# A one-core encoder layer: the value projection turned from token-major to feature-major, and the last two down steps of the last block taken token tile by token tile

## The reference

```python
h = rmsnorm(x, g_pre_mix)
q, k, v, u, g = split_projection(h, w_in)            # q 1024, k 128, v 128, u_a/u_b 1024 each, gates 2048
attn = sink_attention(q, band(k), band(v), rel_bias, valid, sink)   # window 128 + own chunk of 64, 2 kv heads
conv = silu(layernorm(depthwise_conv31(u) + b_dw)) @ w_conv_out
x = x + rmsnorm((g[0] * attn + g[1] * conv) @ w_out, g_post_mix)
h = rmsnorm(x, g_pre_ffn)
y = x + rmsnorm((silu(h @ w_ffn_gate) * (h @ w_ffn_up)) @ w_ffn_down, g_post_ffn)
```

## Time and profile before

| | |
|---|---|
| median of 3 runs | 3476.5 us (3476.41 to 3479.43) |
| the profiled execution | 3481.69 us |
| its span, first to last instruction | 3479.9 us |
| PE busy | 3326.8 us (96% of the span) |
| DVE, ACT, POOL busy | 46%, 29%, 10% |
| mean granted TensorE clock | 0.968 of full |

### The profile page before, as it was taken

The page is one execution under the profiler, slowest core; times in us unless marked ns, Lnnn a source line. Parts: engine busy times, 40 slices in busy tenths (PEclk is TensorE's granted clock), DMA queues, the critical chain, the costliest instruction groups (busy, mean ns, idle before and its releaser), DMA issues.

```text
span 3479.9 us, 42929 instructions
## 1 busy us (share of the span) xinstructions
PE 3326.8 (96%) x17118; PEld 2804.2 (81%) x17118; DVE 1597.9 (46%) x2873; ACT 993.2 (29%) x1830; POOL 358.2 (10%) x422
## 2 busy tenths in 40 slices
PE   7999889999999999999999999999999998899997
PEld 6777668878787878888787878888799987799985
DVE  5977645545785642003594552003397554300012
ACT  2536432224244421003144432002223532200021
POOL 0620000000161000000061000000044000100000
PEclk9999789999999999999999999999999997999998
DMA  7754257777653345555553344555554321355542
GB/s 235 297 221 175 86 194 293 285 277 288 218 182 133 109 157 175 189 199 200 206 194 133 117 148 161 192 193 201 193 178 160 110 86 61 138 182 170 179 147 104
DMA packets 177894, 623.29 MB, mean 179 GB/s; under 512 B 20592, under 2 KB 28080, under 8 KB 177184
## 3 DMA queue, kind: packets, MB, share of 16 engines
q1 hardware_dynamic: 176736, 620.15, 50.6%
q10 hardware_dynamic: 960, 0.40, 0.0%
HBM read 481.13 MB, written 139.44 MB: 178 GB/s over the span
## 4 chain that ended last, share of the span: by engine, by line
PE 71%; issue 6%; DVE 4%; POOL 2%; ACT 2%; DMA 2%; SPq 0%; DVEq 0%; POOLq 0%; ACTq 0%
PE PS L695 42%; PE PS L749 6%; PE PS L751 6%; PE PS L750 6%; PE PS L731 2%; PE PS L821 2%; POOL y L640 1%; DVE PS L1333 1%; PE PS L809 1%; DMA w_hi<-hi_dram 1%; PE PS L810 1%; PE PS L811 1%; PE PS L838 1%; PE PS L839 1%; PE PS L840 1%
## 5 line engine op out<-in xcount | busy, mean ns | idle before, releaser
L695 PE MATMUL PS<-h_hi,w_hi 128*128 128x512 f32 (+1 forms) x3288 | 1052.0, 353 | 18.2 <-DVE u L1542 10.8
L695 PE MATMUL PS<-h_hi,w_lo 128*128 128x512 f32 (+1 forms) x3288 | 1053.3, 353 | 0.0
L695 PE MATMUL PS<-h_lo,w_hi 128*128 128x512 f32 (+1 forms) x3288 | 1043.7, 350 | 0.0
L695 PEld LDWEIGHTS PS<-h_hi,w_hi 128*128 128x128 f32 x3288 | 579.1, 189 | 100.3 <-issue 15.7
L695 PEld LDWEIGHTS PS<-h_lo,w_hi 128*128 128x128 f32 x3288 | 579.1, 189 | 90.8 <-issue 2.2
L695 PEld LDWEIGHTS PS<-h_hi,w_lo 128*128 128x128 f32 x3288 | 579.1, 189 | 81.2
L1333 DVE SCALAR_TENSOR_TENSOR PS<-u,dw,PS 128x512 f32<-128x512 f32 (+1 forms) x696 | 485.8, 767 | 2.9
L1685 DVE TENSOR_TENSOR f<-PS,tmp 128x512 f32<-128x512 f32 (+1 forms) x88 | 61.6, 700 | 669.6 <-PE PS L695 650.7
L640 POOL TENSOR_TENSOR y<-y,prod 128x512 f32<-128x512 f32 (+1 forms) x240 | 289.8, 1239 | 405.9 <-ACT prod L1103 405.9
L749 PE MATMUL PS<-w_hi,f_hi 128*128 128x512 f32 x748 | 297.9, 398 | 5.8 <-DVE f L1685 5.4
L751 PE MATMUL PS<-w_hi,f_lo 128*128 128x512 f32 x748 | 295.8, 395 | 0.0
(11 more groups left out here) (185 smaller groups left out, 4096.8 us busy)
## 6 DMA issues: line engine op xcount, KB each, us to landing
w_lo<-lo_dram SPq DMA_DIRECT2D x372, 512.0 KB, 4.5
w_hi<-hi_dram SPq DMA_DIRECT2D x372, 512.0 KB, 3.6
w_raw<-in_w_stream SPq DMA_DIRECT2D x124, 512.0 KB, 3.9
hi_dram<-w_hi SPq DMA_DIRECT2D x124, 512.0 KB, 4.0
lo_dram<-w_lo SPq DMA_DIRECT2D x124, 512.0 KB, 4.0
x<-in_x_prompt SPq DMA_DIRECT2D x4, 2048.0 KB, 10.7
out_y_prompt<-x SPq DMA_DIRECT2D x4, 2048.0 KB, 7.1
xs<-in_x_prompt SPq DMA_DIRECT2D x12, 512.0 KB, 5.4
```

Source lines behind the costliest of these rows:

```text
L695: last = nc.tensor.matmul(PS[:, k0 + off, 0:n], w, x[:, k, c0:c0 + n], start=first and k == 0, stop=stop and k == KT - 1)
```

## The change

**Step 25** becomes a `feature_major` step like its neighbours. ACT copies its result (features on partitions) from PSUM to `tmp[:, 1]`; PE turns it with one transpose for each token tile (`turn_values`) into PSUM banks 6 and 7; ACT and DVE then take `v_hi` and `v_lo` from there. The turn stands behind the matmuls of step 26 in blocks 0 to 2. In the ext block banks 6 and 7 hold conv accumulators, so it stands behind step 29, after a wait for all taps. The sums of `kwin` move with it from iteration 26 to iteration 30 of DVE, and to another place in SBUF (that of `prod`, so they wait for POOL's last addition); their stores move from SP's iteration 28 to 31, and the wait for these goes from DVE (step 30) to ACT (second attention unit).

**Steps 122 and 123 of the ext block** are held back and run together in `down_tail`: for each token tile its 6 matmuls of step 122, then its 6 of step 123. `d_done` releases ACT's square of each tile when that tile is complete, and `store_y` issues one DMA for each tile.

```diff
-        kwin = at("kwin", R_sc, [P, 2, P])
-        kwin_s = at("kwin_s", R_sc + 2 * P * 4, [P, 2, P])
+        kwin = at("kwin", R_pt, [P, 2, P])
+        kwin_s = at("kwin_s", R_pt + 2 * P * 4, [P, 2, P])
...
+        def turn_step(b):
+            return S_A + 3 if ext(b) else S_A
...
             def store_y(b):
-                m = post_tile(b, tiles(b) - 1, 1)
-                sp.wait_ge(pn_ok, m + 1)
+                if ext(b):
+                    for tt in range(4):
+                        sp.wait_ge(pn_ok, post_tile(b, tt, 1) + 1)
+                        r0 = b * T + tt * P
+                        sp.dma_start(y_prompt[r0:r0 + P, :], x1[:, tt, :]).then_inc(y_out, 16)
+                    sp.wait_ge(pn_ok, post_tile(b, 4, 1) + 1)
+                    sp.dma_start(y_sample, x1[SR:P, 4, :]).then_inc(y_out, 16)
+                    return
...
-                    if ext(b) and s == S_A + 2:
+                    if ext(b) and s == turn_step(b) + 2:
                         sp.wait_ge(win_ok, 4)
...
-                result_out(pe, b, s - 2)
+                if s == S_A + 1:
+                    pe.wait_ge(v_sb_ok, b + 1)
+                else:
+                    result_out(pe, b, s - 2)
...
-            def values_of(b, s):
...
+            def down_tail(b):
+                for tt in range(tiles(b)):
+                    for s in (NS - 2, NS - 1):
+                        dd = s - S_D
+                        if tt == 0:
+                            weights(G(b, s))
+                            pe.wait_ge(flo_ok, b * FT + dd + 1)
+                        for kk in range(2):
+                            last = token_products(b, s, S_D, f_hi[:, dd % 2], f_lo[:, dd % 2], (0, 1), HALF_D,
+                                                  kk, tt)
+                        if tt == tiles(b) - 1:
+                            last.then_inc(w_used, 1)
+                    if tt < tiles(b) - 1:
+                        last.then_inc(d_done, 1)
+
+            def turn_values(b):
+                pe.wait_ge(v_sb_ok, b + 1)
+                for tt in range(tiles(b)):
+                    last = nc.tensor.transpose(PS[:, 6 + tt // 4, (tt % 4) * P:(tt % 4 + 1) * P],
+                                               tmp[:, 1, tok0(b, tt):tok0(b, tt) + P], ident_sb[:])
+                last.then_inc(vt_done, 1)
...
-                    if s < S_A - 1:
+                    if s < S_A:
                         if b or s >= 2:
                             feature_major(b, s, h_hi, h_lo, groups(b))
-                    elif s == S_A - 1:
-                        values_of(b, s)
                     elif s < first_unit(b):
                         feature_major(b, s, h_hi, h_lo, groups(b))
+                        if s == turn_step(b):
+                            if ext(b):
+                                pe.wait_ge(conv_step, (b + 1) * NTAP)
+                            turn_values(b)
...
                     if kind == "v":
-                        zv = PS[:, zbank(b, r), :].rearrange("p (t a d) -> p t a d", t=4, a=2)
+                        A(over(b, tmp[:, 1, 0:c]), z(b, r), ACT.Copy).then_inc(v_sb_ok, 1)
+                    if r == turn_step(b):
+                        act.wait_ge(vt_done, b + 1)
                         if ext(b):
-                            zw = PS[:, zbank(b, r) + 1, 0:P].rearrange("p (a d) -> p a d", a=2)
-                            A(v_hi[:, 5, 0:3:2, :], zw, ACT.Copy)
-                        A(v_hi[:, 1:5, 0:3:2, :], zv, ACT.Copy).then_inc(kv_hi_ok, 1)
+                            A(v_hi[:, 5, 0:3:2, :], PS[:, 7, 0:P].rearrange("p (a d) -> p a d", a=2), ACT.Copy)
+                        A(v_hi[:, 1:5, 0:3:2, :], PS[:, 6, :].rearrange("p (t a d) -> p t a d", t=4, a=2),
+                          ACT.Copy).then_inc(kv_hi_ok, 1)
...
+                            if n == 1 and ext(b):
+                                act.wait_ge(win_out, 16 * 6)
...
                 for tt in range(tiles(b)):
+                    if ext(b) and tt < tiles(b) - 1:
+                        act.wait_ge(d_done, tt + 1)
+                    else:
+                        act.wait_ge(w_used, G(b, NS - 1) + 1)
                     post_squares(b, tt, 1)
...
                         if ext(b):
-                            dve.wait_ge(z_dve, by_dve(b, r))
+                            dve.wait_ge(z_dve, by_dve(b, S_A - 1))
+                            dve.wait_ge(prod_used, NB * NPROD)
...
-                            dve.wait_ge(win_out, 16 * 6)
                         dve.wait_ge(mu_done, b + 1)
```

More of the change, by code:

```diff
@@ L197, in build @@
         o_done, w_gain_ok = sem("o_done"), sem("w_gain_ok")
+        d_done = sem("d_done")
         sq0_ok = sem("sq0_ok")
@@ L217, in build @@
         kv_hi_ok, hist_ok = sem("kv_hi_ok"), sem("hist_ok")
+        v_sb_ok, vt_done = sem("v_sb_ok"), sem("vt_done")
         dve_chain, pool_chain, act_chain = sem("dve_chain"), sem("pool_chain"), sem("act_chain")
@@ L518, in store_y @@
             def store_y(b):
-                m = post_tile(b, tiles(b) - 1, 1)
-                sp.wait_ge(pn_ok, m + 1)
+                if ext(b):
[6 more added lines that the diff above has]
+                    return
+                sp.wait_ge(pn_ok, post_tile(b, tiles(b) - 1, 1) + 1)
                 sp.dma_start(y_prompt[b * T:(b + 1) * T, :].rearrange("(t p) d -> p t d", p=P),
                              x1[:, 0:4, :]).then_inc(y_out, 16)
-                if ext(b):
-                    sp.dma_start(y_sample, x1[SR:P, 4, :]).then_inc(y_out, 16)
             def load_x0(tt):
@@ L582, in _ @@
             store_y(NB - 1)
-            sp.wait_ge(y_out, 16 * (NB + 1))
+            sp.wait_ge(y_out, 16 * (NB - 1 + 5))
             sp.wait_ge(win_out, 16 * 8)
@@ L776, in out_tail @@
                         last.then_inc(o_done, 1)
-            def values_of(b, s):
-                g, k0 = G(b, s), zbank(b, s)
-                weights(g)
-                result_out(pe, b, s - 2)
+            def down_tail(b):
                 for tt in range(tiles(b)):
[L784 to L791, removed]
+                    for s in (NS - 2, NS - 1):
[16 more added lines that the diff above has]
+                last.then_inc(vt_done, 1)
             def scores(b, n):
@@ L903, in _ @@
                         if ln == 3 and ext(b):
-                            pe.wait_ge(conv_step, (b + 1) * NTAP)
                             channel_means(b, ypieces, BY_TAPS + BY_POOL, True, True)
                         if ln == 4:
+                            result_out(pe, b, S_A - 1)
                             channel_squares(b, ypieces)
@@ L968, in _ @@
                             pe.wait_ge(hf_ok, first_norm(b + 1, tiles(b + 1) - 1) + 1)
+                        if ext(b) and s >= NS - 2:
+                            if s == NS - 1:
+                                down_tail(b)
+                            continue
                         pe.wait_ge(flo_ok, b * FT + dd + 1)
@@ L1523, in _ @@
                     kind = KINDS[r] if r >= 0 else None
-                    if kind in BY_DVE:
+                    if kind in BY_DVE and kind != "v":
                         dve.wait_ge(w_used, G(b, r) + 1)
@@ L1548, in _ @@
                            ALU.subtract).then_inc(z_dve, 1)
-                    if kind == "v":
+                    if r == turn_step(b):
                         dve.wait_ge(kv_hi_ok, 2 * b + 2)
                         if ext(b):
-                            zw = PS[:, zbank(b, r) + 1, 0:P].rearrange("p (a d) -> p a d", a=2)
+                            zw = PS[:, 7, 0:P].rearrange("p (a d) -> p a d", a=2)
                             TT(v_lo[:, 5, 0:3:2, :], zw, v_hi[:, 5, 0:3:2, :].bitcast(F32), ALU.subtract)
-                        zv = PS[:, zbank(b, r), :].rearrange("p (t a d) -> p t a d", t=4, a=2)
+                        zv = PS[:, 6, :].rearrange("p (t a d) -> p t a d", t=4, a=2)
                         TT(v_lo[:, 1:5, 0:3:2, :], zv, v_hi[:, 1:5, 0:3:2, :].bitcast(F32),
```

1 line of the change is left out of this document (removed).

## The result

The changed kernel takes 3432.9 us, median of 4 runs (3429.4 to 3437.6), against 3476.5 before: a ratio of 0.9876, 95% interval 0.9859 to 0.9893, or 43.6 us less. The forecast was 34.6 us less, 3441.9 us, with a range from 3438.

A forecast was written before the change was run, and what follows sets the result against it. PE, busy 96% of the span, was taken to bound the kernel. Values steps 14.1 + 6.8 = 20.9 us and tail 13.7 us sum to 34.6 us, from 3476.5 to 3441.9 us, range 3438 to 3448.

The forecast's parts named there:

- Sum: Whole kernel: values-step gain 20.9 plus tail gain 13.7 gives 34.6 us less, 3441.9 us from the median.
- Part A, blocks 0 to 2: Values step: 96 matmuls (10.66 us) become 24 (5.52 us) plus four transposes (0.43 us), gain 4.71 us a block.
- Ext block: Its values step: 13.34 us removed, 6.01 us and five transposes (0.53 us) added, gain 6.80 us.
- both covers: At the ext block's turn: taps finish 7.8 us before PE arrives; PE's means hide the window sums with 2 us to spare.
- Transposes: The 17 new ones in the values steps: 0.106 us each by starts in the trace, against the skill's some 275 ns.
- rival 3: New transposes don't overlap and run one behind the other: 4.1 us more, 3446.0 us; chance 0.05.
- Part B: Tail: last two down steps by token tile with five stores, 13.7 us less at the end of the span.
- the last store: Tail: the final 128 KB store, with nearly empty queues, was taken at 2.3 us, where it had landed in 6.5.
- the 0.4 us in that sum: Tail: added because POOL makes the last tile's factors beside DVE's work, where L615 took 0.59 us and not 0.19.
- rival 1: The longer values step's cover fails and hidden DVE and POOL work comes out: 3447 us, up to 3453; chance 0.10.
- rival 2: The final 128 KB store again takes 6.5 us, so the end is 4.2 us later: 3446 us; chance 0.08.
- rival 4: Slower: ACT's new wait for window stores before the second attention unit lasts over 34.6 us: 3480 us; chance 0.01.

The follow-up runs named there:

- e4: The whole change again, unaltered, timed against the kernel before: 3437.9 us, ratio 0.9882.
- e2: Only the feature-major values step with its transposes, tail and stores as before, against the kernel before: 3447.8 us, ratio 0.9915.
- e6: Kernel before with 42 of the 96 values-step matmuls left out in blocks 0 to 2, against the kernel before: 3456.0 us, ratio 0.9943.
- e9: Kernel before with 12 of the 96 values-step matmuls left out in blocks 0 to 2, against the kernel before: gain 8.0 us (5.6 to 11.8).
- e5: Feature-major values alone, step 25 padded to its old length by overwritten matmuls, against the kernel before: 3478.4 us, ratio 1.0002.
- e11: Kernel before with 19 overwritten matmuls added in block 0's values step, against the kernel before: gain 2.2 us (-0.3 to 5.9).
- e12: The change with last-but-one down step run for token tiles 0 and 1 first, against the kernel before: 3432.2 us, ratio 0.9872.

## Why the prediction missed

**The step that failed is the Sum.** It read "20.9 + 13.7 = 34.6 us. The span becomes 3445.3": everything outside the touched steps was taken to keep its time. It had no term for PE's clock, although the page before gave a mean of 0.968, 0.032 x 3479.9 = 111 us of clock loss in that execution, some 10 of them behind PE's end. The range failed with it: it took "the 1.5 us that runs of one kernel differ by" from three runs, where 17 spread over 16 us. The change moved all work behind step 25 forward, by 5 us at first and by 30 at the end, less of it ran at half speed, and that came to 9.6 us between the two profiles and 5 to 9 us in the medians (39.1 - 34.5 in e4, 43.6 - 34.5 in the first measurement). A us of clock loss isn't worth a us of time everywhere, since PE also waits for others in some of it: in e2 10.6 us less loss stood beside 8.5 us more gain than the matmuls explain, in e6 11.4 beside 7.1, in e9 7.1 beside 4.0.

That it was the place of the work which made the difference is argued from e5, e6 and e9 to e11, by leaving out the form and the length; no run moved the same program in time without changing it.

**Part A, blocks 0 to 2**: right, 4.77 us for 4.71, and PE waits for nothing new. **Ext block**: 6.4 for 6.8; both covers held; `v_lo` and the sums took 2661.01 - 2659.17 = 1.84 us, where the sums alone had taken 3.96. They now wait for POOL's last addition, and in the trace of before POOL was adding beside them (L640, 2666.97 to 2670.81); no run separates that from other causes. The 0.4 us: by the issues of its loads step 25 itself saves 13.34 - 6.05 = 7.29 us, the five transposes cost 0.55 as forecast, and the other 0.3 us went in the steps beside it, 0.05 to 0.08 us in each, the longer steps shown above. **Transposes**: right, 0.09 us each by starts in block 1 and (2658.12 - 2657.57) / 5 = 0.11 in the ext block, which settles rival 3. The Trainium skill (TensorE: Matmul & The Clock Gate, Part 4: PE-mode transpose) has some 275 ns for one in a kernel's context; the trace disagrees, and the measurement decides.

**Part B**: right in its sum. PE's wait 1.36 for 1.35, the last store 3435.8 - 3433.50 = 2.3 us as taken, DVE's last tile 3430.68 - 3428.23 = 2.45 us behind PE's end for 2.5 (PE's end 0.26 us behind the start of its last matmul, as in the window of the earlier trace rows). But the 0.4 us in that sum were right by luck, for they had the wrong reason: POOL isn't slowed (L626 takes 0.19 us), its factors are there at 3430.38, and DVE is busy with the tile before until 3430.64. So DVE only just keeps up, which is what e12 ran into. **Rivals** 1, 2 and 4 didn't come: no cover failed, the small store landed in 1.9 us, and PE waits for nothing at the second attention unit that it didn't wait for before. The rival that was missing is a gain or loss by the clock of what isn't touched.

**What stays open**: which waits will be followed by half speed. The runs show that shifting the work in time changes it while the wait and the work around it stay the same; what in the position counts they don't tell, and give no rule by which a kernel could be placed on purpose. The Trainium skill (TensorE: Matmul & The Clock Gate, Part 1: The HAM clock gate) has the clock follow how busy PE has been of late. The trace agrees in so far as half speed comes behind the 1.03 us wait in the kernel before; that the same wait may be followed by none is what the rows here add.

## What to carry to other kernels

In a kernel bound by PE, a time saved early moves all that follows, and the granted clock of untouched stretches can add or take away as much as a small edit is worth: here 5 to 9 us in 3477. Before costing an edit, read the mean clock and the spread over many runs, give the range that much on both sides, and judge edits of a few us by intervals in the trace (from a landmark to the end), not by the whole time. At the end of a kernel, order by token tile and small last stores are worth having both, and their gains add.

## What the hardware showed that was not expected

- A wait of PE of only 1.03 us was followed by 1.2 GHz in the kernel before and not in the change; with 12 and 42 matmuls cut there was none either, with 31 cut or 19 added it was there.
- Adding 2.1 us of matmuls once lowered the mean clock loss from 99.8 to 95.0 us, and the median from 3476.0 to 3473.9, though that gain alone can't be told from none.
- At the full clock, with PE never idle, the same step of 48 matmuls with 272 columns took 5.97, 6.03 or 6.05 us, each all through the steps ahead of step 25 of the ext block, in kernels with the same work.
- A 128 KB store lands in 1.9 us when nothing is ahead of it and in 6.5 us behind 2 MB; stores of 512 KB, about 2.9 us apart, land in 2.6 us.
